# Output projection's last column block in two passes over token tiles, with the first layer norm's transposes between its tiles and inside the first products

## What is computed

```
def block(x, mod, ...):
    sh1, sc1, g1, sh2, sc2, g2 = jnp.split(mod, 6, axis=-1)
    h = x * (1 + sc1) + sh1
    m, s_f, s_b = mixer(h, ...)          # ends with: mixed @ w_out
    x = layer_norm(ALPHA * x + g1 * m, ln1_g, ln1_b)
    h = x * (1 + sc2) + sh2
    gate, up = jnp.split(h @ w_gu, 2, axis=-1)
    f = (jax.nn.silu(gate) * up) @ w_down
    x = layer_norm(ALPHA * x + g2 * f, ln2_g, ln2_b)
```

## Time and profile before

| | |
|---|---|
| median of 3 runs | 2835.76 us (2835.28 to 2838.61) |
| profiled execution, its own time | 2834.99 us |
| its span | 2833.2 us |
| PE busy | 2705.8 us (96%) |
| PE weight load busy | 2417.2 us (85%) |
| DVE busy | 1398.4 us (49%) |
| ACT busy | 890.3 us (31%) |
| POOL busy | 655.2 us (23%) |
| mean granted TensorE clock | 0.981 of full speed |

### The profile page before, as it was taken

One profiled execution on the slowest core, in us unless ns is written; L12 is line 12 of the kernel. 1 busy time (PEld: TensorE's weight loads), 2 busy tenths in 40 slices (PEclk: granted clock), 3 DMA queues, 4 the chain that ended last, 5 costly groups with the idle time before them and its releaser, 6 DMA issues.

```text
span 2833.2 us, 37694 instructions
## 1 busy us (share of the span) xinstructions
PE 2705.8 (96%) x16304; PEld 2417.2 (85%) x16304; DVE 1398.4 (49%) x1551; ACT 890.3 (31%) x930; POOL 655.2 (23%) x219
## 2 busy tenths in 40 slices
...
GB/s 327 314 242 175 181 176 194 211 154 60 102 146 240 109 87 121 104 98 89 95 99 104 104 104 104 95 88 94 103 104 127 241 182 220 169 204 171 215 168 104
DMA packets 165257, 426.59 MB, mean 151 GB/s; under 512 B 9548, under 2 KB 11988, under 8 KB 158052
## 3 DMA queue, kind: packets, MB, share of 16 engines
...
## 4 chain that ended last, share of the span: by engine, by line
PE 72%; DMA 8%; DVE 7%; POOL 7%; ACT 3%; issue 3%; SPq 0%; POOLq 0%; ACTq 0%; DVEq 0%
PE ps L2006 7%; PE ps L2007 7%; PE ps L2008 7%; PE ps L2082 7%; PE ps L2084 7%; PE ps L2083 7%; PE ps L1755 5%; PE ps L1756 5%; PE ps L1757 5%; PE ps L1808 4%; DMA raw_w<-w_gu_b 4%; PE ps L1735 3%; DMA low<-w_ada 2%; POOL raw_w L818 2%; PE ps L1958 2%
## 5 line engine op out<-in xcount | busy, mean ns | idle before, releaser
L1462 DVE TENSOR_TENSOR w_lo<-raw_w,w_hi 128x1024 fp32r<-128x1024 f32 x264 | 351.4, 1333 | 308.2 <-ACT w_hi L1070 305.5
L1070 ACT ACTIVATE w_hi<-raw_w 128x1024 fp32r<-128x1024 f32 x264 | 269.8, 1054 | 625.8 <-POOL raw_w L824 376.2
L2006 PE MATMUL ps<-x_hi,w_hi 128*128 128x320 f32 x1408 | 436.5, 310 | 3.9 <-DVE w_lo L1462 3.9
L2007 PE MATMUL ps<-x_lo,w_hi 128*128 128x320 f32 x1408 | 435.5, 309 | 0.0
L2008 PE MATMUL ps<-x_hi,w_lo 128*128 128x320 f32 x1408 | 435.5, 309 | 0.0
L1593 DVE TENSOR_TENSOR x_lo<-low,x_hi 128x2560 fp32r<-128x2560 f32 x44 | 216.3, 4915 | 291.2 <-ACT x_hi L1155 291.2
L815 POOL TENSOR_TENSOR low<-raw_w 128x1024 f32<-128x1024 f32 x42 | 104.5, 2488 | 1089.5 <-DMA raw_w<-w_gu_b 1089.5
L1755 PE MATMUL ps<-x_hi,w_hi 128*128 128x320 f32 x1056 | 341.4, 323 | 8.2 <-DVE x_lo L1265 6.2
L2082 PE MATMUL ps<-w_hi,x_hi 128*128 128x512 f32 x880 | 343.2, 390 | 2.2 <-POOL w_lo L829 2.2
L2084 PE MATMUL ps<-w_hi,x_lo 128*128 128x512 f32 x880 | 343.0, 390 | 0.0
L2083 PE MATMUL ps<-w_lo,x_hi 128*128 128x512 f32 x880 | 342.9, 390 | 0.0
...
## 6 DMA issues: line engine op xcount, KB each, us to landing
...
low<-w_ada SPq DMA_DIRECT2D x60, 1024.0 KB, 5.4
...
raw_w<-w_down SPq DMA_DIRECT2D x44, 1024.0 KB, 5.1
raw_w<-w_in_b SPq DMA_DIRECT2D x33, 1024.0 KB, 7.3
high<-w_ada SPq DMA_DIRECT2D x22, 1024.0 KB, 5.3
raw_w<-w_out SPq DMA_DIRECT2D x16, 1024.0 KB, 5.1
x_raw<-w_ada SPq DMA_DIRECT2D x14, 1024.0 KB, 9.0
```

What stands on the lines that cost most here:

```text
L1070: nc.scalar.activation(weight(0, w), src, ACT.Copy).then_inc(prod_hi, 1)
L1462: nc.vector.tensor_tensor(weight(1, n), src, weight(0, n).bitcast(F32), ALU.subtract).then_inc(prod_split, 1)
L2006: mm(out, wh, version(v, 0, k), start=first and k == 0, stop=False)
L2007: mm(out, wh, version(v, 1, k), start=False, stop=False)
```

## The change

The last column block is done in two passes. Units 12 to 15 hold its four weight units for token tiles 0 to 2, and units 16 to 19 load the same four weight units once more for tiles 3 and 4, so there are 20 units in place of 16. PE does the second pass in pieces: units 16 and 17, turns 0 and 1, tile 3 of unit 18, turn 2, tile 4 of unit 18, turn 3, unit 19. Turns 4 to 7 (v and s) stand inside product 0, one pair after every other step. Products 1 to 4 follow, and turns 8 to 15 stand inside products 5 and 6, one pair ahead of every other step. ACT and DVE do the normalisation of tiles 0 to 2 between the splits of units 17 to 19, and that of tiles 3 and 4 after B21. w0, w1, w4, w5, w6 and w7 are split at other places in their lists. The gate rows of the last block are kept at another address, and the s turns 0 to 7 use PSUM banks 7 and 3 in place of 7 and 5.

The core of the diff:

```diff
@@ -45,7 +45,7 @@
 EPS = 1e-5
 UNIT = 2048
 N_IN = 33
-N_OUT = 16
+N_OUT = 20
 SC, SH = 0, 1
 V_OFF, G_OFF, A_OFF, P_OFF = 1024, 2048, 3072, 3104
 K_ARR = 2 * RANK + 1
...
 PLAIN_BANK = ((1, 2), (3, 4), (5, 6), (7, 0))
-TURN_V, TURN_S = (0, 6), (7, 5)
+TURN_V, TURN_S = (0, 6), (7, 3, 7, 5)
+SPLIT = 3
+
+
+def out_unit(i):
+
+    if i < 12:
+        return i // 4, i % 4, (0, TT)
+    return 3, i % 4, ((0, SPLIT) if i < 16 else (SPLIT, TT))
+
+
+def turn_bank_s(a):
+
+    return TURN_S[a % 2 + (0 if a < HK else 2)]
 
 
 def turned_of(engine, a):
...
             load_quad(0, q)
+
+        def store_normed(tiles):
+
+            for t in tiles:
+                sp.wait_ge(ln1_normed, t + 1)
+                sp.dma_start(xn_d[t], u_acc[:, t, :]).then_inc(xn_out, 16)
+
+        store_normed(range(SPLIT))
         load_quad(1, A11)
         load_quad(1, A21)
-        for t in range(TT):
-            sp.wait_ge(ln1_normed, t + 1)
-            sp.dma_start(xn_d[t], u_acc[:, t, :]).then_inc(xn_out, 16)
         load_quad(1, A12)
+        store_normed(range(SPLIT, TT))
         load_quad(1, A22)
         for i in (2, 3):
             for q in PLAIN_Q:
@@ -1096,43 +1134,51 @@
...
-        prod_round(0)
-        prod_round(1)
-        for t in range(TT):
-            act.wait_ge(ln1_moments, t + 1)
-            nc.scalar.activation(mv(t, 2), mv(t, 1), ACT.Sqrt, bias=cols(C_EPS, 1)).then_inc(ln1_rstd, 1)
-            act.wait_ge(ln1_scale, t + 1)
-            nc.scalar.activation(u_acc[:, t, :], u_acc[:, t, :], ACT.Identity, bias=mv(t, 3),
-                                 scale=mv(t, 2)).then_inc(ln1_normed, 1)
+        ln1_root(0)
+        ln1_normalise(0)
+        split_in(N_IN + 17)
+        ln1_root(1)
+        ln1_root(2)
+        ln1_normalise(1)
+        split_in(N_IN + 18)
+        ln1_normalise(2)
+        split_in(N_IN + 19)
         act.wait_ge(folded, 5)
         for a in range(4):
             fold_s(a)
         act.wait_ge(folded_s, 4)
-        act.wait_ge(out_evac, OUT_ACC)
+        act.wait_ge(out_evac, 3 * TT + SPLIT)
         round_version(whole(B11, 0)[:, second], h11[:, second])
+        prod_round(0)
+        prod_round(1)
         act.wait_ge(unit_used, FU)
         for a in range(4, HK):
             fold_s(a)
+        prod_round(2)
         act.wait_ge(folded_v, HK)
         round_version(whole(B21, 0)[:, first], h21[:, first])
         act.wait_ge(folded_s, HK)
         round_version(whole(B21, 0)[:, second], h21[:, second])
-        prod_round(2)
         prod_round(3)
+        ln1_root(3)
+        ln1_normalise(3)
+        ln1_root(4)
+        prod_round(4)
+        ln1_normalise(4)
+        prod_round(5)
         for a in range(HK, 2 * HK):
+            if a == HK + 4:
+                prod_round(6)
             fold_s(a)
+        prod_round(7)
         act.wait_ge(turned_v, 2 * HK)
         act.wait_ge(xn_out, 16 * TT)
         act.wait_ge(folded_v, 2 * HK)
         round_version(whole(B12, 0), by_token(h12))
-        prod_round(4)
-        prod_round(5)
         act.wait_ge(folded_s, 2 * HK)
         round_version(whole(B22, 0), h22)
-        prod_round(6)
         act.wait_ge(t_formed, 1)
         silu_plain(0)
-        prod_round(7)
         act.wait_ge(t_formed, 3)
         act.wait_ge(ver_split, 5)
         round_version(whole(T2, 0), raw_version(T2))
@@ -1466,50 +1512,62 @@
...
+        evac_out(3, 0)
+        ln1_scales(0)
+        evac_out(3, 1)
+        evac_out(3, 2)
+        ln1_scales(1)
+        split_rest(N_IN + 17)
+        ln1_scales(2)
+        split_rest(N_IN + 18)
 
...
@@ -1546,37 +1604,45 @@
 
         dve.wait_ge(folded, 5)
         first, second = slice(0, VER // 2), slice(VER // 2, VER)
-        for a in range(4):
-            fold_v(a)
+        fold_v(0)
+        fold_v(1)
+        split_rest(N_IN + 19)
+        fold_v(2)
+        fold_v(3)
         dve.wait_ge(folded_v, 4)
-        dve.wait_ge(out_evac, OUT_ACC)
+        dve.wait_ge(out_evac, 3 * TT + SPLIT)
         link(nc.vector.tensor_copy(whole(B11, 0)[:, first], h11[:, first]))
         version_rest(whole(B11, 1)[:, first], h11[:, first], whole(B11, 0)[:, first], 0)
+        prod_rest(0)
+        version_rest(whole(B11, 1)[:, second], h11[:, second], whole(B11, 0)[:, second], 1)
+        prod_rest(1)
         dve.wait_ge(unit_used, FU)
-        fold_v(4)
-        fold_v(5)
-        version_rest(whole(B11, 1)[:, second], h11[:, second], whole(B11, 0)[:, second], 1)
-        fold_v(6)
-        fold_v(7)
+        for a in range(4, HK):
+            fold_v(a)
         version_rest(whole(B21, 1)[:, first], h21[:, first], whole(B21, 0)[:, first], 2)
+        prod_rest(2)
         version_rest(whole(B21, 1)[:, second], h21[:, second], whole(B21, 0)[:, second], 3)
-        prod_rest(2)
+        evac_out(3, 3)
         prod_rest(3)
+        ln1_scales(3)
+        evac_out(3, 4)
+        ln1_scales(4)
+        prod_rest(4)
+        prod_rest(5)
         for a in range(HK, 2 * HK):
+            if a == HK + 4:
+                prod_rest(6)
             fold_v(a)
+        prod_rest(7)
         dve.wait_ge(folded_v, 2 * HK)
         dve.wait_ge(turned_s, 2 * HK)
         dve.wait_ge(xn_out, 16 * TT)
+        version_rest(whole(B12, 1), by_token(h12), whole(B12, 0), 4)
         difference(raw_version(T1), by_token(h12), by_token(h11))
-        prod_rest(4)
-        prod_rest(5)
         dve.wait_ge(folded_s, 2 * HK)
         difference(raw_version(T3), h22, h12)
         dve.wait_ge(t_formed, 1)
         difference(by_token(raw_version(T2)), by_token(h22), raw_version(T1))
-        prod_rest(6)
-        version_rest(whole(B12, 1), by_token(h12), whole(B12, 0), 4)
-        prod_rest(7)
         dve.wait_ge(t_formed, 3)
         version_rest(whole(B22, 1), h22, whole(B22, 0), 5)
         difference(raw_version(T4), by_token(raw_version(T2)), by_token(h21))
@@ -1937,31 +2003,35 @@
...
+        for i in range(18):
+            for t in range(*out_unit(i)[2]):
+                out_tile(i, t)
...
@@ -1992,12 +2062,15 @@
             if a >= 2:
                 pe.wait_ge(folded_s, a - 1)
             else:
-                pe.wait_ge(out_evac, OUT_ACC)
-            turn_half(TURN_S[a % 2], *turned_of("s", a)).then_inc(turned_s, 1)
+                pe.wait_ge(out_evac, 3 * TT + SPLIT)
+            turn_half(turn_bank_s(a), *turned_of("s", a)).then_inc(turned_s, 1)
...
         def product(out, w, v, n, first, last):
 
             for k in range(HK):
+                if (n, k) in TURN_AT:
+                    turn_v(TURN_AT[n, k])
+                    turn_s(TURN_AT[n, k])
...
 
-        pe.wait_ge(ln1_normed, 3)
-        for a in (0, 2, 4):
-            turn_v(a)
-            turn_v(a + 1)
-            turn_s(a)
-            turn_s(a + 1)
-        plain(0)
-        turn_v(6)
-        turn_v(7)
-        turn_s(6)
-        turn_s(7)
-        plain(1)
-        pe.wait_ge(ln1_normed, TT)
-        for a in range(HK, 2 * HK):
-            turn_v(a)
-            turn_s(a)
-        for n in range(2, N_PLAIN):
+        TURN_AT = {(0, 1): 4, (0, 3): 5, (0, 5): 6, (0, 7): 7}
+        TURN_AT.update({(5 + i // 4, 2 * (i % 4)): HK + i for i in range(HK)})
+
+        pe.wait_ge(ln1_normed, SPLIT)
+        turn_v(0)
+        turn_s(0)
+        turn_v(1)
+        turn_s(1)
+        for t in range(SPLIT, TT):
+            out_tile(18, t)
+            turn_v(t - 1)
+            turn_s(t - 1)
+        for t in range(SPLIT, TT):
+            out_tile(19, t)
+        for n in range(N_PLAIN):
+            if n == 5:
+                pe.wait_ge(ln1_normed, TT)
             plain(n)
```

132 lines of the change are left out of this document (70 added, 62 removed).

## The result

| | before | after |
|---|---|---|
| median | 2835.15 us (20 runs, 2831.89 to 2840.14) | 2844.68 us (20 runs, 2839.36 to 2847.20) |
| ratio | | 1.0033, 95% interval 1.0027 to 1.0039 |
| profiled execution, its span | 2834.99, 2833.2 | 2847.20, 2845.4 |
| mean granted clock | 0.981 | 0.979 |

The change costs 9.5 us. The profiled execution after is the longest of its 20, and it reaches the split of the last block's second unit 3.96 us later than the execution before does (1018.87 against 1014.91). That part lies ahead of everything the change touches and differs from run to run in all kernels. To compare two traces behind it, I take the 3.96 off; such a time is marked "on before's scale".

The account below looks back on a forecast made before the run. PE, busy 96%, was taken to bound the kernel, with a DVE tail behind the last turn; w11's remainder 5.0 late plus 0.9 for bunched loads put product 18 5.9 late: 2840.9, median 2841.7 us, range 2835.5 to 2852.

Parts of the forecast that it names:

- the +4 to +8: Main forecast for the whole program: 4 to 8 us slower than the kernel before, given 50%.
- a short low clock: Clock rival's mild case: one or two short pieces ahead of the last turn run slow, 2 to 4 us, 2845.
- PE's early waits: PE waits at unit 17 and products 2, 3, 4 and 6, ahead of the last turn, 7.3 us together.
- The last turn: End of PE's 32 turns: 1110.7 without waits, 1118.0 with them, against about 1108.5 before.
- The tail: From last turn to w8's remainder: ACT's folds and roundings, six DVE passes, remainders; 30.3 us, ready at 1148.3.
- The load burst: Four quarter loads ahead of product 18 start within 4 us, not 3.5 apart; cost 0 to 2.6, taken 0.9.
- The clock did not fall in the interleaved stretches: Rival: turns inside products pull the clock down, some 11 us, 2852.7, or 2845 if briefly; 23% together.
- The early waits did not vanish: Rival: the 7.3 us of waits ahead of the last turn mostly vanish; 2833.5 at best, partial forms around 2837.5; 24%.
- the tail doesn't bind: Rival: w8 is ready before PE needs it, product 12 begins at 1136.3, 8.5 us earlier, 2827 us; 3%.
- the rule that I weighed: Transposes may not engage the full clock; interleaved turns were priced at the high level all the same, 0.56 us each.

Follow-up runs that it names:

- e8: Changed kernel with w6's rounding and remainder ahead of folds 8 to 15 instead of between folds 11 and 12; 2837.31 us, ratio 1.0022.
- e1: Changed kernel with turns 8 to 15 all inside product 5, one pair ahead of each step, instead of products 5 and 6; 2838.27 us, ratio 1.0015.
- e5: Changed kernel with turns 8 to 15 in product 5, w8-w11 remainders ahead of T2's and T3's, and T1 ahead of w7 and B12; 2828.29 us, ratio 0.9985.
- e6: Kernel before with w8 to w11's remainders ahead of those of T2 and T3 on DVE, nothing else; 2833.19 us, ratio 1.0004.
- e10: Kernel before with turns 8 to 15 inside product 2 and w8 to w11's remainders ahead of T2's and T3's; 2839.67 us, ratio 1.0026.
- e3: Changed kernel with difference T1 ahead of w7's remainder and B12's version on DVE; 2841.04 us, ratio 1.0022.
- e9: Kernel before with turns 8 to 15 inside product 2, without the second pass; 2839.01 us, ratio 1.0026.
- e12: Kernel before with turns 8 to 15 inside product 3, so product 2 runs undisturbed; 2840.15 us, ratio 1.0009.

## Why the prediction was right

The forecast was "slower", 2841.7 us with a sum of +5.9; the result is 2844.68, +9.5. The mechanism is the one forecast, two terms were too small. The result lies within the range of 2835.5 to 2852 but outside the +4 to +8 that I gave one half, close to the 2845 that I had put down for a short low clock, which is not what brought it there: both stretches of interleaved turns ran at 1.00 in the trace.

- **PE's early waits.** Forecast 1.3, 1.9, 1.4, 1.7 and 1.0 (unit 17, products 2, 3, 4, 6), measured 0.99, 1.57, 1.06, 1.36 and 2.04, together 7.3 against 7.0. The last was mis-sized: I wrote that PE does turn 12 and is there first; in the order of the program product 6 waits for w6 ahead of turn 12, so the wait stood in the way of the last four pairs of turns, and it was twice as long. e8 took it away, and the last folds came 2.1 earlier.
- **The last turn.** Forecast 1118.0, measured 1119.9, though the waits' sum was right. What the sum lacked is what a wait costs beyond its row. From product 2 to product 3 it is 1097.46 - 1092.62 = 4.84, and a product (3.52) and the listed wait (1.06) make 4.58: 0.26 more. A row counts idle time from a matmul's modelled end, 0.31 behind its start, where the next could have started 0.15 behind it, and the first matmul behind a wait takes 0.25 in place of 0.15. Five waits: 1.3. A switch from turns to matmuls costs the second half of it (a tile with two turns behind it takes 3.95, from 1065.64 to 1069.59, where the sum has 3.84; in the products it is less), in all 14 places some 0.8. Together 2.1, less 0.3 for the waits: 1.8 of the 1.9.
- **The tail.** Forecast 30.3 from the last turn to w8's remainder. Measured: 1123.86 to 1153.02 + 1.2, 30.3. The six passes in a row, product 10 waiting for B22 (3.9 forecast, 3.80 found) and product 12 for w8 came as forecast. Product 12 waited 3.67 and not 5.6, as PE arrived late, having run products 10 and 11 partly at the low clock behind the 3.80; like PE's waits at products 7 and 10, that cost nothing, as PE was still 1.93 early at product 18. The waits ahead of the last turn are another matter: they moved the turn and with it the tail (e8).
- **The load burst.** Forecast between 0 and 2.6, taken 0.9; found 2.4 (6.3 against 3.9). I chose the value nearer nothing because a load was rarely alone before either. The traces speak for a larger one: from issue to landing the four loads take 5.9 in the median after and 4.5 before, and with w8 to w10 in one piece the way from w11's remainder to POOL takes 5.4 to 6.3 (after, e1 to e5, e8), with the four 3.5 apart 3.8 (e6, e10), and from 3.9 to 5.1 for forms between. With 2.4 and the true last turn, the sum gives 5.9 + 1.9 + 1.5 = 9.3, and product 18 was 9.4 late.
- **The rivals.** The clock did not fall in the interleaved stretches (1.00 at 1076 and 1104), so that rival fell here. It was a real one, and in part it was luck that this trace shows none of it: e3, with the same PE instructions, lost 1.4 us to it ahead of the last turn, and e9 all of product 2. How many of the changed kernel's 20 runs had such a fall isn't known. The early waits did not vanish. That the tail doesn't bind is refuted by the waits for it, 3.67 at product 12 and 1.93 at product 18.

On the rule that I weighed (the Trainium skill, "TensorE: Matmul & The Clock Gate", part 4: transposes don't count as PE-busy the way matmuls do): the changed kernel's turns kept 1.00 in both stretches, and e1's and e12's did so with two turns to every step. By this alone the rule would seem wrong. In e9 it agrees with the trace: the same mixture, PE never idle, didn't bring a fallen clock back in 20 us, where e12's unmixed product did. With turns only ahead of every second step, as in the changed kernel, e3's clock came back within the mixture, after some 3 us.
